# A hybrid HGRN2 and Fourier block: the position codes of token tiles 4 to 15 added on GpSimd instead of VectorE

## What is computed

```python
def sincos_2d(length, dim):
    ...
    return jnp.concatenate([axis_code(row), axis_code(col)], axis=-1)

def rmsnorm(x, w):
    xf = x.astype(F32)
    y = xf * lax.rsqrt(jnp.mean(xf * xf, axis=-1, keepdims=True) + EPS)
    return (y * w.astype(F32)).astype(x.dtype)

def reference(x, c, ctx, c_ctx, ...):
    x = x + sincos_2d(length, d).astype(x.dtype)[None]
    ...
    shift, scale, gate = jnp.split(sc @ w_ada[l] + b_ada[l], 3, axis=-1)
    hx = rmsnorm(x, norm_w[l]) * (1.0 + scale[:, None]) + shift[:, None]
    out_x, _, _ = mix_stream(hx, w_in[l], ...)
    x = x + gate[:, None] * out_x
    return rmsnorm(x, final_norm_w)
```

## Time and profile before

| | us |
|---|---|
| median of 3 runs | 2251.25 |
| lowest and highest | 2251.05, 2253.62 |
| the profiled execution | 2252.65 |
| its span in the profile | 2250.9 |

### The profile page before, as it was taken

How to read it: one execution, slowest core, us unless ns; L and a number is a source line. 1 busy time by engine, 2 the same in 40 slices (tenths; PEclk the granted TensorE clock), 3 DMA queues, 4 the chain that set the end, 5 groups by cost and what they waited for, 6 DMA issues and landing times.

```text
span 2250.9 us, 48635 instructions
## 1 busy us (share of the span) xinstructions
PE 2166.8 (96%) x20832; PEld 1814.4 (81%) x20832; DVE 1497.7 (67%) x3209; ACT 510.8 (23%) x838; POOL 73.5 (3%) x106
## 2 busy tenths in 40 slices
PE   7799999999999999999999999999997989999997
PEld 3799988788788888888887888778786877888886
DVE  4865754125777767787777777688887776656464
ACT  3721133101111211112121121111113343222221
POOL 0000102000000000000000000000000000000000
PEclk9999999999999999999999999999997999999999
DMA  8534554333324233423333243323335357444551
GB/s 287 178 118 145 186 154 158 118 125 94 106 86 135 90 121 95 127 93 110 103 95 125 83 129 102 117 90 117 98 101 189 136 204 245 154 164 134 170 173 57
DMA packets 232809, 298.84 MB, mean 133 GB/s; under 512 B 14826, under 2 KB 159882, under 8 KB 230290
## 3 DMA queue, kind: packets, MB, share of 16 engines
q1 hardware_dynamic: 148386, 178.33, 24.6%
q10 hardware_dynamic: 73952, 81.18, 10.6%
q0 software_dynamic: 10256, 36.21, 5.0%
HBM read 198.11 MB, written 97.56 MB: 131 GB/s over the span
## 4 chain that ended last, share of the span: by engine, by line
PE 89%; DVE 5%; DMA 2%; issue 2%; ACT 1%; SPq 1%; ACTq 0%; POOL 0%; DVEq 0%
PE all_bank L61 25%; PE all_bank L63 23%; PE all_bank L62 23%; PE all_bank L1461 3%; PE all_bank L1462 2%; PE all_bank L1453 2%; PE all_bank L1407 2%; PE all_bank L1423 2%; PE all_bank L1436 1%; PE all_bank L1446 1%; DVE hidden_h_lo L474 1%; PE all_bank L1041 1%; PE all_bank L996 1%; PE all_bank L2511 1%; DMA front_w_mod<-in_w_ada 1%
## 5 line engine op out<-in xcount | busy, mean ns | idle before, releaser
L61 PE MATMUL all_bank<-hidden_h_hi,head_hi 128*128 128x512 f32 x1184 | 491.0, 415 | 4.5 <-issue 4.3
L63 PE MATMUL all_bank<-hidden_h_hi,head_lo 128*128 128x512 f32 x1184 | 465.6, 393 | 0.0
L62 PE MATMUL all_bank<-hidden_h_lo,head_hi 128*128 128x512 f32 x1184 | 463.2, 391 | 0.0
L1499 ACT ACTIVATE head_projected<-all_bank 128x512 f32<-128x512 f32 x148 | 88.6, 598 | 870.2 <-PE all_bank L63 870.2
L63 PEld LDWEIGHTS all_bank<-hidden_h_hi,head_lo 128*128 128x128 f32 x1184 | 222.5, 188 | 51.8
L61 PEld LDWEIGHTS all_bank<-hidden_h_hi,head_hi 128*128 128x128 f32 x1184 | 222.9, 188 | 49.6 <-issue 4.4
L62 PEld LDWEIGHTS all_bank<-hidden_h_lo,head_hi 128*128 128x128 f32 x1184 | 223.4, 189 | 39.7
L1584 DVE RECIPROCAL head_inverse<-head_gate 128x448 f32<-128x448 f32 x64 | 186.0, 2933 | 0.0
L1625 DVE TENSOR_TENSOR head_query<-head_query,head_total 128x256 f32<-128x256 f32 x256 | 108.4, 423 | 103.4 <-PE all_bank L1423 73.7
L61 PE MATMUL all_bank<-front_hi,hidden_h_hi 128*128 128x256 f32 x512 | 143.8, 281 | 0.0
L63 PE MATMUL all_bank<-front_hi,hidden_h_lo 128*128 128x256 f32 x512 | 142.7, 279 | 0.0
(11 more groups left out here) (285 smaller groups left out, 4251.6 us busy)
## 6 DMA issues: line engine op xcount, KB each, us to landing
head_raw<-in_w_in POOLq DMA_DIRECT2D x37, 512.0 KB, 4.9
head_value<-value_rows SPq DMA_DIRECT2D x64, 256.0 KB, 5.2
head_query<-piece_query SPq DMA_DIRECT2D x64, 256.0 KB, 6.8
head_out<-head_o ACTq DMA_DIRECT2D x64, 256.0 KB, 5.5
tail_o<-head_out SPq DMA_DIRECT2D x32, 512.0 KB, 6.0
front_raw<-in_w_in SPq DMA_DIRECT2D x19, 512.0 KB, 5.2
front_w_mod<-in_w_ada SPq DMA_DIRECT2D x8, 1024.0 KB, 14.0
front_stage<-in_x SPq DMA_DIRECT2D x16, 512.0 KB, 8.9
```

Source lines behind the costliest of these rows:

```text
L61: nc.tensor.matmul(out, st_hi, mv_hi, start=start, stop=False)
L62: nc.tensor.matmul(out, st_hi, mv_lo, start=False, stop=False)
L63: return nc.tensor.matmul(out, st_lo, mv_hi, start=False, stop=stop)
L1499: nc.scalar.activation(projected[unit % 2][:], ps_proj[unit % 2][:], PIECES[name][1], scale=PIECES[name][2]).then_inc(proj_copied, 1)
```

## The change

GpSimd adds the codes of tiles 4 to 15, in tile order, each as soon as the tile's two DMAs have landed. It counts them in a new semaphore, `coded_late`. `wait_coded` picks the semaphore that a tile's code is counted in; SyncE and ScalarE use it. VectorE keeps the codes of tiles 0 to 3. Its order becomes `split_rows(0)`, norms 4 to 7, `split_rows(1)`, norms 8 to 11, `split_rows(2)`, norms 12 to 17, `split_rows(3)`.

```diff
+    def wait_coded(engine, t):
+        if t < TPG:
+            engine.wait_ge(coded, t + 1)
+        else:
+            engine.wait_ge(coded_late, t - TPG + 1)
...
     @block.gpsimd
...
         pool.memset(there[:, GRP:GRP + 1], 0.0).then_inc(row_set, 1)
+        pool.wait_ge(col_in, P // GRID_W * DMA)
+        for t in range(TPG, NT):
+            pool.wait_ge(x_in[t], 2 * DMA)
+            pool.tensor_tensor(xs[t][:, 0:H], xs[t][:, 0:H], rows[t][:], ALU.add)
+            pool.tensor_tensor(xs[t][:, H:D], xs[t][:, H:D], col[:], ALU.add).then_inc(coded_late, 1)
         for i in range(PAIRS):
...
         for t in range(8, 12):
-            sp.wait_ge(coded, t - 3)
+            wait_coded(sp, t - 4)
             load_x(t)
...
         for t in range(12, NT):
-            sp.wait_ge(coded, t - 3)
+            wait_coded(sp, t - 4)
             load_x(t)
...
         split_rows(0)
-        code(4)
-        for t in range(5, 8):
-            code(t)
-            norm(t - 1)
-        code(8)
-        norm(7)
+        for t in range(4, 8):
+            norm(t)
         split_rows(1)
-        for t in range(9, 12):
-            code(t)
-            norm(t - 1)
-        code(12)
-        norm(11)
+        for t in range(8, 12):
+            norm(t)
         split_rows(2)
-        for t in range(13, NT):
-            code(t)
-            norm(t - 1)
-        norm(NT - 1)
+        for t in range(12, NT):
+            norm(t)
...
     def _(act):
         def root(t):
             if t < NT:
-                act.wait_ge(coded, t + 1)
+                wait_coded(act, t)
```

More of the change, by code:

```diff
@@ L282, in front @@
          "gate_raw", "scan_done", "weighed", "key_turned", "key_t_copied", "s_done", "s_copied"))
-    (row_set, mid_folded, mid_cleared, mid_high_done, mid_ready, summed, paired, w_folded, w_high_done, w_low_done, token_high_done, token_low_done, step_done,
+    (row_set, mid_folded, mid_cleared, mid_high_done, mid_ready, summed, paired, coded_late, w_folded, w_high_done, w_low_done, token_high_done, token_low_done, step_done,
      mid_copied, mid_stored) = (r.sem(n) for n in (
-         "row_set", "mid_folded", "mid_cleared", "mid_high_done", "mid_ready", "summed", "paired", "w_folded", "w_high_done", "w_low_done", "token_high_done",
+         "row_set", "mid_folded", "mid_cleared", "mid_high_done", "mid_ready", "summed", "paired", "coded_late", "w_folded", "w_high_done", "w_low_done", "token_high_done",
          "token_low_done", "step_done", "mid_copied", "mid_stored"))
```

## The result

The kernel after takes 2258.15 us in the median of 13 executions (2255.65 to 2263.38), the kernel before, timed beside it on the same chip, 2251.15 us in 13 (2247.02 to 2256.51). The ratio is 1.0032, with a 95% interval of 1.0023 to 1.0042: slower by 5 to 9.5 us, with 2259.9 predicted. The profiled execution after took 2258.14 us, its span 2256.4.

What follows compares the result with a forecast made beforehand. It took TensorE to bound the kernel (89% of the chain), so first-stage changes move the end equally. Terms 11.8 + 0.5 - 3.7 gave +8.6 us, 2259.9 against the median of 2251.25; range 2253 to 2268.

Steps and rivals of the forecast that it cites:

- The turns of the two engines: Split of group 0: VectorE and GpSimd instructions never work at once; a block takes 3.12 us instead of 1.06.
- (a): Before group 0's split: GpSimd does three additions while VectorE would idle, at no cost.
- the sum: Whole first stage: 11.8 + 0.5 - 3.7 = +8.6 us; chance of the forecast 0.62.
- (b): Split of group 0: taking turns with additions makes values 0 end at 71.1 instead of 59.3, +11.8 us.
- (c): Norms of group 1: four multiplications take turns with four additions, 7.0 us; values 1 another 0.5 us later.
- (d): Group 2: values 1 to values 2 stays 17.3 us from start to start, effect 0.
- (e): Group 3: ScalarE's roots no longer wait for codes and end at 98.8 instead of 102.46, -3.7 us.
- Casts do not pass freely: Rival on VectorE's casts and multiplications: they pass freely, only subtractions take turns; 2245.9 us, chance 0.11.
- GpSimd gets in behind a cast of 0.29: Rival in the splits denied this: two VectorE instructions to one of GpSimd, block 1.98 us; 2254.2 us, chance 0.13.
- The dearer addition: Rival on GpSimd's additions: a turn of 1.61 us, a block of 4.06; 2270 us, chance 0.08.
- The rival without contention: GpSimd's additions cost VectorE nothing: -3.2 us in group 1, -6.9 with group 3; 2244.3 us, chance 0.06.

Runs made afterwards that it cites:

- the kernel without additions: The change with the additions of tiles 4 to 15 left out on all engines, GpSimd only signalling by a one-column memset: 2241.66 us, ratio 0.9961.
- the woven kernel: Kernel before, nothing on GpSimd; VectorE adds all codes, moved ahead of splits and behind blocks 4, 5 and 6 of the preceding split: 2241.07 us, ratio 0.9962.

## Why the prediction was right, point by point

- **The turns of the two engines.** Right. A block of the split takes 3.10 against 3.12 summed, made of the four turns 0.29, 1.14, 0.55 and 1.14. That they come from GpSimd's additions running beside VectorE, and from nothing else in the change, is shown from both sides: additions that nobody reads do the same to VectorE, and without additions the loss is gone.
- **(a), three additions ahead of the split.** Two were done by the first cast (the second ended at 44.34, 0.16 into it), and the third, from 44.31, fell into the split. From the end of VectorE's weight subtraction, which held GpSimd's first addition up to 2.59, to the first cast there were 2.23 us in this execution (41.95 to 44.18) and not the 3.43 of the sum's. It cost nothing ahead of the split, as said. So one addition more was left over at the end, and the first cast (1.25) and subtraction (1.65) of group 1's split met the last two.
- **(b), +11.8.** Right: values 0 is over 12.2 later than before, the last subtraction at 23.83 against 23.8. TensorE's last step took 1.8 behind the last subtraction. The sum names 1.37 for it, but its 71.1 has 1.5 in it; by its own terms it is 71.0. The clock did not fall in the starved stretch.
- **(c), +0.5.** Right in the place where it ends, 36.19 against 36.1, with some luck in its parts. The four multiplications with their additions took 6.7 instead of 7.0 (30.54 - 23.83), and from the last norm to values 1 were 5.65 us instead of 5.3. Measured from the end of values 0, the term is 0.2.
- **(d), 0.** Mis-sized by 0.8: values 1 to values 2 took 16.46 instead of 17.28. The sum took the first evacuation as coming directly behind values 1 in both kernels. Before, it came directly behind group 2's last root, which the codes had held up; after, with the roots done early, it waited only for the product's first banks. ScalarE's timelines, before and after:

```profile
81.06 0.29 ACT L695 ACTIVATE front_stat<-front_stat,front_eps 128x1 f32<-128x1 f32 x1
81.27 0.36 ACT L724 ACTIVATE front_out<-all_bank 128x256 f32<-128x256 f32 x1
```

```profile
90.88 0.39 ACT L727 ACTIVATE front_out<-all_bank 128x256 f32<-128x256 f32 x1 [1.25 <-PE all_bank L63]
```

  Values 1 was over at 80.97 and 91.36, so the evacuation came 0.3 behind that point before and 0.5 ahead of it after. The product itself took 11.39 us in the first execution before and 10.99 in the second, and both have the evacuation at 35.46 and values 2 at 41.05 from the first cast: it was the root and not the product that counted. It is the mechanism of (e), in a group where the sum did not look for it, and the kernel without additions has it too (0.9 in group 2).
- **(e), -3.7.** Right: 21.76 instead of 25.45, with the roots freed of the codes.
- **The sum.** +7.9 in the stage, +8.6 predicted; the difference is (d). In the median +7.0, with an interval of 5.2 to 9.5 that holds both.
- **The rivals.** Casts do not pass freely, and GpSimd gets in behind a cast of 0.29, since each block has two additions. The dearer addition did not come. The size of the rival without contention was too small: 6.9 us, where the stage of the kernel without additions is 9.8 shorter (in the median, 2244.3 against 2241.7, the interval would allow both). It kept the evacuation behind values 0 and the low clock up to values 1, and left out what the roots give back in group 2.

What stays open: the 2.5 us that the woven kernel gained in the median beyond its stage, the 4 us by which executions of one kernel differ behind values 3, and why additions and copies hand the path over after each instruction and memsets don't. That the memsets carry no read is a difference between the two, and no run here shows that it is the reason.

## What to carry to other kernels

An elementwise instruction that is given from VectorE to GpSimd costs VectorE its turn: here 0.61 of VectorE became 1.14 of GpSimd, in which VectorE could not do a cast, a multiplication or a subtraction either. In this kernel it would have paid only where VectorE was idle or doing nothing that anyone waited for; that GpSimd was free said nothing. Look first whether VectorE has slack of its own at another place of its list: the same 24 additions, moved in between the blocks of a split that ran ahead of TensorE, made the kernel 5 to 12 us faster, where GpSimd made it 5 to 9.5 slower.

## What was not expected of the hardware

- 58 memsets of 128x512 on end on GpSimd held a VectorE copy of 128x16 for 24.30 us; additions and copies on GpSimd let VectorE in after each one.
- A subtraction with two inputs runs at its 0.69 beside a memset; a cast waits for it (0.74 instead of 0.43).
- On GpSimd an addition of one tile with itself is cheaper (0.86 to 0.97 a turn) than one of two tiles (1.09 to 1.20), a copy 0.43 to 0.54, a memset 0.46, all of 128x512.
- TensorE kept a granted clock of 1.00 over 10 us in which it was busy for half the time (4.98 us), in steps 3.1 us apart.
- Two executions of the kernel before agreed to 0.01 us over the 66.50 of the stage, while their spans differed by 5.9.
